# Two chained blocks on one core: layer norm earlier, gate logarithm on another engine, beta out of the delta stage's matmuls, norm roots and filler reordered

## The reference, cut to what matters

```python
def layer_norm(x, w, b, eps=LN_EPS):
    mu = jnp.mean(xf, axis=-1, keepdims=True)
    xc = xf - mu
    y = xc * lax.rsqrt(jnp.mean(xc * xc, axis=-1, keepdims=True) + eps)

    beta = jax.nn.sigmoid(b_in)
    g = -jnp.exp(a_log) * jax.nn.softplus(a_in + dt_bias)

    g = jnp.cumsum(g, axis=-1)
    decay = jnp.exp(jnp.where(causal, g[..., :, None] - g[..., None, :], -jnp.inf))
    kb = k * beta[..., None]
    lower = jnp.where(strict, jnp.einsum('bhnid,bhnjd->bhnij', kb, k) * decay, 0.0)
    rhs = jnp.concatenate([v * beta[..., None], kb * jnp.exp(g)[..., None]], axis=-1)
    sol = lax.linalg.triangular_solve(tri, rhs, left_side=True, lower=True, unit_diagonal=True)
```

## Time and profile before

| | us |
|---|---|
| three runs | 2547.42, 2547.82, 2549.56 |
| median | 2547.82 |
| profiled execution's own time | 2549.82 |
| its span, first to last instruction | 2548.0 |
| PE busy / POOL / ACT / DVE | 2484.7 / 1455.7 / 1246.3 / 1171.3 |
| mean granted PE clock | 0.993 of full |

### The profile page before, as it was taken

One profiled execution on the slowest core, in us unless ns is written; L12 is line 12 of the kernel. 1 busy time (PEld: TensorE's weight loads), 2 busy tenths in 40 slices (PEclk: granted clock), 3 DMA queues, 4 the chain that ended last, 5 costly groups with the idle time before them and its releaser, 6 DMA issues.

```text
span 2548.0 us, 42067 instructions
## 1 busy us (share of the span) xinstructions
PE 2484.7 (98%) x16588; PEld 2170.4 (85%) x16588; DVE 1171.3 (46%) x2176; ACT 1246.3 (49%) x2113; POOL 1455.7 (57%) x835
## 2 busy tenths in 40 slices
PE   7998999999999899999999999999999999999998
PEld 7997989888999788898777877778888878898998
DVE  8896645444878645536415613331101123535144
ACT  6467654355546764436544522443323345636543
POOL 6875746456977664544533343646565546464970
PEclk9999999999999899999999999999999999999999
DMA  6543343345544344335421022232222233235554
GB/s 244 180 167 145 133 166 134 139 175 182 182 173 160 131 156 154 121 137 206 175 83 66 34 83 81 89 116 90 92 99 95 88 116 127 82 140 193 188 182 149
DMA packets 50601, 347.63 MB, mean 136 GB/s; under 512 B 5361, under 2 KB 8689, under 8 KB 8945
## 3 DMA queue, kind: packets, MB, share of 16 engines
q1 hardware_dynamic: 47840, 340.31, 37.1%
q10 hardware_dynamic: 2576, 4.72, 0.6%
HBM read 343.96 MB, written 1.05 MB: 135 GB/s over the span
## 4 chain that ended last, share of the span: by engine, by line
PE 91%; DVE 4%; ACT 3%; issue 1%; POOL 1%; DMA 1%; ACTq 0%; DVEq 0%; SPq 0%; POOLq 0%
PE pg L1948 23%; PE pg L1950 23%; PE pg L1949 23%; PE ps L2266 2%; PE pg L1971 2%; PE ps L2287 2%; PE ps L2285 1%; PE ps L2423 1%; PE ps L2404 1%; PE ps L2117 1%; ACT ring_hi L778 1%; PE ps L2123 1%; PE ps L2092 1%; PE ps L2504 1%; PE ps L2497 1%
## 5 line engine op out<-in xcount | busy, mean ns | idle before, releaser
L663 POOL TENSOR_TENSOR ring_lo<-ring,ring_hi 128x1024 fp32r<-128x1024 f32 (+3 forms) x502 | 1169.9, 2345 | 705.8 <-ACT ring_hi L778 704.8
L1948 PE MATMUL pg<-HH,ring_hi 128*128 128x256 f32 (+1 forms) x3264 | 1038.7, 318 | 8.1 <-POOL ring_lo L663 5.9
L1949 PE MATMUL pg<-HH,ring_lo 128*128 128x256 f32 (+1 forms) x3264 | 992.2, 304 | 0.0
L1950 PE MATMUL pg<-HL,ring_hi 128*128 128x256 f32 (+1 forms) x3008 | 920.0, 306 | 0.0
L1948 PEld LDWEIGHTS pg<-HH,ring_hi 128*128 128x128 f32 x3264 | 619.2, 190 | 73.8 <-issue 36.9
L1949 PEld LDWEIGHTS pg<-HH,ring_lo 128*128 128x128 f32 x3264 | 619.4, 190 | 43.4 <-issue 16.5
L1950 PEld LDWEIGHTS pg<-HL,ring_hi 128*128 128x128 f32 x3008 | 570.5, 190 | 28.3
L778 ACT ACTIVATE ring_hi<-ring 128x1024 fp32r<-128x1024 f32 (+3 forms) x572 | 563.8, 1003 | 30.3 <-DMA ring<-in_w_stream_dram 22.3
L788 ACT ACTIVATE take<-pg 128x256 f32<-128x256 f32 (+1 forms) x242 | 103.7, 429 | 452.6 <-PE pg L1950 445.0
L1950 PE MATMUL pg<-big_r,ring_hi 128*128 128x256 f32 (+1 forms) x928 | 299.3, 323 | 0.0
L1948 PE MATMUL pg<-big_r,ring_hi 128*128 128x256 f32 (+1 forms) x752 | 246.0, 327 | 3.9 <-DVE ring_lo L1633 2.7
(11 more groups left out here) (350 smaller groups left out, 3337.7 us busy)
## 6 DMA issues: line engine op xcount, KB each, us to landing
ring<-in_w_stream_dram SPq DMA_DIRECT2D x320, 1024.0 KB, 4.8
hn<-in_consts_dram ACTq DMA_DIRECT2D x2, 1024.0 KB, 6.0
cst<-in_consts_dram SPq DMA_DIRECT2D x1, 1472.0 KB, 19.5
prm<-in_params_dram SPq DMA_DIRECT2D x1, 1110.0 KB, 9.3
X<-in_xT_dram SPq DMA_DIRECT2D x1, 1024.0 KB, 5.8
X<-in_ctxT_dram ACTq DMA_DIRECT2D x1, 1024.0 KB, 5.9
out_dram<-H ACTq DMA_DIRECT2D x4, 256.0 KB, 2.2
cst<-in_consts_dram SPq DMA_DIRECT2D x1, 768.0 KB, 16.5
```

The source lines that it names most:

```text
L663: pool.tensor_tensor(ring_lo[:, slot, cols], ring[:, slot, cols], ring_hi[:, place * P:(place + n) * P].bitcast(F32), SUB).then_inc(sem(LO ...
L1948: first = pe.matmul(out, a[0], b[0], start=start, stop=False)
L1949: pe.matmul(out, a[1], b[0], start=False, stop=False)
L1950: return first, pe.matmul(out, a[0], b[1], start=False, stop=stop)
```

## The change

**Delta net.** The matrix `IB`, its eight matmuls (four units, two layers) and `pre_beta` go. `pre_keys` multiplies the key products by beta and decay with four 128x128 DVE instructions, each with beta as a per-partition scalar; beta of the values goes into ACT's copies (`VN`, each cut in two), and `VB` becomes one plain DVE copy. `diagonals` halves. `GAPS` is set anew, and the parts are placed by their length in matmuls; chunks `dz`, `az` and `a_out` are cut into eight parts of three matmuls instead of four of six.

**Layer norm.** Centring moves ahead of the short convolution of chunk 20, the square ahead of the drain of `dn` chunk 22, the reduce ahead of the short convolution of chunk 22.

**Gates.** `delta_log` moves to POOL as nine linked 128x16 instructions after the second `c_out` merge; its reciprocal becomes an Exp on ACT. The triangular matmul moves from the second attention step to the fill of step 12 and writes to a `pg` bank.

**Norms.** In norms 1, 2, 4, 5, 6 and 7 the table load stands ahead of the last square. In norms 1 and 6 one of two weight roundings stands ahead of the root and the second behind it. `pair()` runs high products first; the second chunk's low-weight products come last, as one block. `HL` follows `H` one step sooner. One more `ring_lo` at the start goes to DVE.

```diff
-GAPS = [0.4, 1.0] + [1.9, 0.3] * 4 + [1.9, 0.7] + [1.6, 1.1, 1.0, 0.2]
+GAPS = [0.4, 1.0, 1.7, 0.3, 1.7, 0.9] + [1.7, 0.3] * 2 + [1.9, 0.7] + [1.6, 1.1, 1.0, 0.2]
...
-    return {"modt": 1}.get(name, 4)
+    return {"modt": 1, "dz": KD, "az": KD, "a_out": KD}.get(name, 4)
...
+            def delta_log(l):
+                pool.wait_ge(sem("over_abs"), l + 1)
+                link(pool.tensor_scalar(NGC, B1, 1.0, None, ADD))
...
+                pool.tensor_scalar(G, B0, -1.0, None, MUL).then_inc(sem("g_done"), 1)
...
                     merge("c_out", l, m, True)
+                    if m == 1:
+                        delta_log(l)
...
+                    if m == KD + 1:
+                        log_exp_tables()
                     if m >= 2:
                         norm_square(i, m - 2)
...
+                act.activation(GC, B2, ACT.Exp, scale=-1.0).then_inc(sem("over_abs"), 1)
...
-                act.activation(VN[:, 0:2 * P], ps[:, 2, 2 * P:4 * P], ACT.Copy).then_inc(sem("d_vn0"), 1)
+                for hh in range(2):
+                    ins = act.activation(VN[:, hh * P:(hh + 1) * P], ps[:, 2, (2 + hh) * P:(3 + hh) * P], ACT.Copy,
+                                         scale=BETA[:, 0, 2 * u + hh:2 * u + hh + 1])
...
-                dve.wait_ge(sem("d_lb"), i + 1)
-                dve.tensor_tensor(LTS[u % 2], ps[:, 0 if u else 2, :], LTS[u % 2], MUL).then_inc(sem("d_lt"), 1)
+                dve.wait_ge(sem("d_exp"), i + 1)
+                for p in range(4):
+                    h, c = 2 * u + p // 2, p % 2
+                    s = slice(p * P, (p + 1) * P)
+                    ins = dve.scalar_tensor_tensor(LTS[u % 2][:, s], ps[:, 0 if u else 2, s], BETA[:, c, h:h + 1], DTS[u % 2][:, s], MUL, MUL)
+                ins.then_inc(sem("d_lt"), 1)
...
-                    pe.matmul(dst, ones, IB, start=True, stop=True).then_inc(sem("d_ib"), 1)
...
-                    if 2 <= v <= 5 and u < UNITS - 1:
+                    if v in (2, 4, 5) and u < UNITS - 1:
```

More of the change, by code:

```diff
@@ L212, in delta_fill @@
         parts += [("part", x)] * (n_parts(x[0]) - 1) + [x]
-    parts.insert(4, parts.pop(0))
+    parts.insert(KD, parts.pop(0))
+    work = [{"mod": 8, "modt": 16}.get((x[1] if x[0] == "part" else x)[0], 6) for x in parts]
     gaps = DELTA_START + GAPS * (UNITS - 1) + LAST_GAPS
     out = [[] for _ in gaps]
-    at, end = 0, gaps[0]
-    for k, x in enumerate(parts):
-        while sum(gaps) * (k + 0.5) / len(parts) > end:
+    at, end, done = 0, gaps[0], 0
+    for x, w in zip(parts, work):
+        while sum(gaps) * (done + w / 2) / sum(work) > end:
             at += 1
             end += gaps[at]
+        done += w
         out[at].append(x)
@@ L522, in build @@
         DT1, LT1, IN1 = (cut(at_buf, 1536 + j * PAIRS, PAIRS) for j in range(3))
-        VB, UG, IB, VN = (cut(big, 6144 + j * PAIRS, PAIRS) for j in range(4))
+        VB, UG, VN = (cut(big, 6144 + j * PAIRS, PAIRS) for j in (0, 1, 3))
         LM = [LM0, LM1]
@@ L1362, in norm_over @@
                 dve.wait_ge(sem("norm_rms"), i + 1)
-                for k in range(KD + 2):
+                for k in range(KD + 1):
                     if k < KD:
@@ L2379, in _ @@
                 fill(delta_fill(l)[0])
-                for step in range(4):
+                for step in (0, 2, 3):
                     delta_pre(l, 0, step)
```

193 lines of the change are left out of this document (98 added, 95 removed).

## The result

| | before | after |
|---|---|---|
| median of runs, us | 2547.82 | 2536.06 |
| lowest to highest of five, us | 2547.42 to 2549.56 | 2534.18 to 2538.69 |
| profiled execution's own time, us | 2549.82 | 2534.18 |
| its span, us | 2548.0 | 2532.3 |
| PE busy in it, us | 2484.7 | 2473.4 |

The ratio is 0.9949 (95% interval 0.9938 to 0.9961): 11.8 us faster by the medians, where 35.5 were forecast, and 2536 lies above the range. In the profiled executions (after's is its fastest run; their mean granted clocks are 0.993 and 0.996) it is 15.6: 11.3 less of PE's busy time, and 4.4 less of its idle time (span less busy: 63.3, then 58.9). The forecast wanted at least 15 of idle time, so by its own mark it falls.

A forecast was written before the change was run, and what follows sets the result against it. PE was taken as the bound (91% of the last-ending chain), so gains come from fewer instructions, less idle time and less half-speed time. Terms -7.5 + 1.0 - 3.9 - 10.8 - 9.5 - 2.0 - 2.0 - 0.5 - 0.3 = -35.5: 2512 us, range 2503 to 2529.

The forecast's parts named there:

- so I take nothing: Gates: nine `delta_log` instructions handed to POOL were given no cost, with 4.4 us a layer as the bad end.
- about 1.0 of wait stays: Gates: of PE's 7.6 us of waits over two layers, about 1.0 stays per layer, so 5.6 go.
- The third rival: Gates: POOL is late with nine instructions of 0.74, leaving 4.4 us a layer to PE; 2521 us, chance 5%.
- Next late would be the drains of `cz` and the row of the modulation: Behind the layer norm: these come just ahead of PE; cost taken as nothing, bad end 2.5 us a layer.
- the rival of a chain that binds: Delta stage: bound by its chain because the eight removed matmuls were also cover; 2521 us, at worst 2530, chance 12%.
- Four rounds fewer: Delta stages' finer filler: 56 rounds of modulation matmuls instead of 60, at 0.86 to 1.05 us each, giving -3.9.
- but the next chunk's ring_lo, made after the last `HH`, stops the gain at 2.6: Norm 1: the earlier root gains between 1.1 and 2.6 us, capped by this low part; -2.0 taken.
- takes short waits away, -0.3: Pairs of chunks behind the norms: the new order with low products last removes short waits, -0.3 us.
- the clock and passed-on waits: Rival: waits are only passed on and the clock falls anyway, at gates, modulation row and norms; 10 us, 2522, chance 20%.
- The rival that ends slower: Delta stage: copies or subtractions 0.4 us late at each of 96 PE waits, 38 us in all; 2551 us, chance 4%.
- The marks named: Signs of being right: reduce and gate-sum waits gone, clock near 1.00 behind layer norms, norm 1 and 6 waits 1.2 to 1.5.
- the marks set down for "wrong": PE waiting on L1612 or L999 successors, `ring_lo` in attention, or modulation rows after layer norm; or unchanged half-speed stretch at gates.

The follow-up runs named there:

- e4: Kernel before with the gates part alone (logarithm on POOL, triangular matmul in step 12, beta's steps in step 13): 2553.0 us, ratio 1.0018.
- e11: Kernel before with the gates part, beta's affine step on ACT, and the low parts of a layer's first two `c_out` chunks on DVE: 2537.29 us, ratio 0.9957.
- e3: Kernel before with the layer norm's centring, square and reduce moved, alone: 2543.65 us, ratio 0.9981.
- e17: Kernel before with table loads ahead of the last square and one rounding behind the root in norms 1 and 6, alone: 2550.93 us, ratio 1.0006.
- e10: Kernel before with the delta stage's part alone (no `IB` matmuls, new `GAPS`, finer filler, `VN` scaled in its copies): 2544.53 us, ratio 0.9975.
- all four together: After with the old pair order, plus beta on ACT, `c_out` `ring_lo` on DVE, modulation row first, and norms 1 and 6 mended: 2523.59 us, ratio 0.9896.

## Why the prediction was right and wrong

The direction was right, and the mechanisms that it named are in the trace. The size was three times too large, and the time lies above the range. By parts, each alone on before:

| part | forecast | measured alone (interval) | at 0.994 |
|---|---|---|---|
| 1 and 2, delta stage | -10.4 | -6.4 (-8.9 to -3.6) | -7.8 |
| 3, layer norm | -10.8 | -4.8 (-7.1 to -2.5) | -6.6 |
| 4, gates | -9.5 | +4.6 (+2.3 to +6.9) | +3.0 |
| 5, roots | -4.5 | +1.5 (-0.8 to +3.8) | +0.3 |
| 5, pair order | -0.3 | +5.1 (+2.5 to +7.4) | +4.9 |
| sum | -35.5 | 0.0 | -6.2 |
| the change | | -13.0 (-15.8 to -9.9) | -9.2 |

That the whole is better than the sum is mostly the clock (after's runs have a mean of 0.995, the five single parts 0.992 to 0.993); the 3 that remain at equal clock are less than the intervals are wide. One edit, the `ring_lo` given to DVE at the start, was not run alone; PE's waits in the first 60 us are 16.4 in before and 16.1 in after, so it is near the nothing that was set down.

- **Part 4 carried most of the error.** The failing step is "so I take nothing" for POOL, and "about 1.0 of wait stays" as the only wait behind the gates; behind the new waits the clock falls as it had behind the old ones, so the 3.9 for it isn't won in e4 either. The third rival, POOL late by 4.4 a layer, had the right engine and about the right price (3.6 a layer for `at_buf` and `XL` beyond the 1.0), with the wrong instructions: the nine of `delta_log` run from 275.12 to 277.91 in after, 2.8 in all, and no wait of PE leads to them. What is late is the doubling of z, which the change doesn't touch. It took 4.6 a step on an engine without slack, and the old wait for the gates had been its cover. The rule of the Trainium skill (GPSIMD Engine Reference, section 4.1, Engine selection) that the forecast weighed against the move was not what decided. The other half is one instruction of beta that moved to another step, and for which the forecast has no term; there it runs into POOL's rounding and lasts 2.3, as L1499 had done before in a place where PE waited for the gates anyway. e11, without both, gave -11.0 against -9.5 (-6.2 at equal clock). Why e4 is slower and not merely no faster stays open.
- **Part 3**: timing of the centring, the square and the reduce was right to within a microsecond, and both 3.3 waits went. The step that failed is "Next late would be the drains of `cz` and the row of the modulation that ACT makes behind them ... I take nothing for them, and 2.5 a layer as the bad end". The row came 0.9 late in both layers, and the clock fell there instead, in e3 in both layers, in after in layer 0: the 1.7 won behind the layer norm was lost again ten us on. The bad end was the true one, 10.8 - 2 x 2.5 = 5.8 against 4.8 measured (6.6 at equal clock).
- **Parts 1 and 2**: the direction and the absence of a large stall were right; the rival of a chain that binds was not what happened. The `IB` matmuls were worth 0.85 each, the lower end of the forecast (6.8 against 6.9 to 8.2). The step that failed is "Four rounds fewer": the traces have two fewer, worth 2.2 and not 3.9. And the waits were 2.7 instead of 1.0.
- **Part 5, roots**: "but the next chunk's ring_lo, made after the last `HH`, stops the gain at 2.6" had the right instruction and the wrong place. The low part comes so late that nothing is left, as e17 shows: 1.5 + 2.0 of wait for 2.9. Norm 7 gave its 0.5: in after the shift grows from -15.2 at its sum to -15.7 at the end.
- **Part 5, pairs**: "takes short waits away, -0.3" is the step with the wrong sign. It looked at the waits and not at the pace: with DVE at 1.57 a block, the low products had been the filler. That cost +5.
- **The rivals**: the clock and passed-on waits, 20% and 2522, was the true family of causes, but was priced at 10, from the clock at the gates, the row of the modulation and the norms' low ends; the waits for `XL` and behind beta's step, the `ring_lo` of norms 1 and 6 and the pairs' tail aren't in it. The rival that ends slower (96 waits in the delta stage) has no trace: PE's waits there are five, of 0.2 to 1.1, in e10.
- **The marks named**: the reduce and the gate sums off the list, clock 1.00 behind both layer norms, 1.0 before the third scores (in e11; in after 1.3 in layer 1 and none in layer 0), waits of 1.2 to 1.5 for `HH`: all seen. Also seen were three of the marks set down for "wrong": the modulation rows after the layer norm, POOL in the attention (with `XL`, not `ring_lo`), and, at 0.2 twice, a successor of L999 in the delta stages. And PE's idle time is 4.4 lower, not 15.

## What to carry to other kernels

A wait that goes is a cover that goes: before counting it as gain, look for the next engine without idle time in the same stretch and take its work per step (POOL: three of 0.74 and one of 2.38) against the new pace of the engine that no longer waits. Moving work behind a stream that is paced by another engine removes filler; compare both paces per block (1.40 against 1.57) and not only the waits in the list. The gains of single mends didn't add up (all four together gave no more than one of them), so undo and mend one at a time, and read the place of each wait again after every step.
